# Expert stages of a two-block model: refills of the first weight slots issued in three parts, and one slot's place in the order of loads

## The reference, cut to what matters

```python
# hier_moe on n tokens h (512 tokens in layer 0, 256 in layer 1), top 2 experts of the best group
for each expert e and its tokens x:
    y = (silu(x @ w1[e]) * (x @ w3[e])) @ w2[e]
    out[token] += gate[token, e] * y
```

## Time and profile before

| | us |
|---|---|
| runs | 2123.81, 2121.19, 2123.91 (median 2123.81) |
| profiled execution | 2121.46, span 2119.7 |
| PE busy | 1903.6 (90% of the span) |
| DVE busy | 983.7 (46%) |
| DMA traffic | 610.65 MB, mean 288 GB/s |
| stage 0 of the experts | about 1035 to 1498 |
| stage 1 of the experts | about 1674 to the end |

### The profile page before, as it was taken

One profiled execution on the slowest core, in us unless ns is written; L12 is line 12 of the kernel. 1 busy time (PEld: TensorE's weight loads), 2 busy tenths in 40 slices (PEclk: granted clock), 3 DMA queues, 4 the chain that ended last, 5 costly groups with the idle time before them and its releaser, 6 DMA issues.

```text
span 2119.7 us, 22003 instructions
## 1 busy us (share of the span) xinstructions
PE 1903.6 (90%) x8957; PEld 1034.6 (49%) x8957; DVE 983.7 (46%) x1781; ACT 316.5 (15%) x717; POOL 37.7 (2%) x52
## 2 busy tenths in 40 slices
PE   8999999998999999999999999999999955455557
PEld 5558874455588745884643333333456511111112
DVE  3238878466378795646433333333765410110111
ACT  2121110226211103011200000000234200000000
POOL 0000000000000000000100000000000000000000
PEclk9999999999999999999999999999999977777789
DMA  9347886451278864421899999999722899999998
GB/s 367 137 142 265 288 297 219 146 184 41 81 270 285 296 222 161 138 101 40 345 429 426 427 426 426 427 427 423 276 80 99 313 425 427 426 426 426 427 426 338
DMA packets 147686, 610.65 MB, mean 288 GB/s; under 512 B 14609, under 2 KB 65489, under 8 KB 123136
## 3 DMA queue, kind: packets, MB, share of 16 engines
q1 hardware_dynamic: 141920, 595.87, 71.7%
q0 software_dynamic: 5568, 13.24, 1.7%
q10 hardware_dynamic: 96, 0.10, 0.0%
HBM read 610.62 MB, written 4.33 MB: 290 GB/s over the span
## 4 chain that ended last, share of the span: by engine, by line
PE 78%; DMA 15%; DVE 3%; ACT 2%; issue 1%; SPq 1%; DVEq 0%
PE psum L1071 14%; PE psum L2701 14%; PE psum L524 9%; PE psum L2729 7%; DMA ring<-in_w 6%; PE psum L1011 6%; PE psum L2766 5%; PE psum L1890 4%; DMA arena<-in_w 4%; DMA consts<-in_w 3%; PE psum L566 3%; PE psum L1977 2%; DMA normed_t<-in_w 1%; PE psum L642 1%; PE psum L1366 1%
## 5 line engine op out<-in xcount | busy, mean ns | idle before, releaser
L1071 PE MATMUL psum<-normed_t,ring 128*128 128x256 f32 x1408 | 306.4, 380 | 0.0
L1071 PEld LDWEIGHTS psum<-normed_t,ring 128*128 128x128 f32 x1408 | 266.9, 190 | 43.5 <-issue 7.2
L2701 PE MATMUL psum<-ring,arena 128*32 128x512 f32 (+1 forms) x720 | 211.0, 670 | 63.3 <-DMA arena<-in_w 24.6
L923 DVE SCALAR_TENSOR_TENSOR arena<-ring,silu_c,arena 128x1024 f32<-128x1024 f32 x168 | 204.7, 1279 | 0.0
L524 PE MATMUL psum<-ring,normed_t 128*128 128x512 f32 x448 | 196.7, 596 | 2.1 <-issue 0.9
L3136 DVE TENSOR_TENSOR resid<-resid,psum 128x512 f32<-128x512 f32 x160 | 109.9, 688 | 184.5 <-PE psum L2766 184.5
L2701 PE MATMUL psum<-consts,arena 128*32 128x512 f32 (+1 forms) x288 | 146.9, 669 | 19.5 <-DMA arena<-in_w 19.5
L3144 DVE TENSOR_TENSOR scaled<-scaled,psum 128x512 f32<-128x512 f32 x24 | 16.5, 688 | 315.8 <-PE psum L2701 315.8
L524 PEld LDWEIGHTS psum<-ring,normed_t 128*128 128x128 f32 x448 | 84.0, 191 | 104.1 <-issue 103.2
L2701 PE MATMUL psum<-arena 128*32 128x512 f32 (+1 forms) x328 | 108.2, 651 | 28.7 <-DMA ring<-in_w 28.7
L2701 PEld LDWEIGHTS psum<-ring,arena 128*32 128x32 f32 (+1 forms) x720 | 56.5, 131 | 142.6 <-issue 142.6
(11 more groups left out here) (570 smaller groups left out, 2805.3 us busy)
## 6 DMA issues: line engine op xcount, KB each, us to landing
ring<-in_w SPq DMA_DIRECT2D x96, 2048.0 KB, 29.8
arena<-in_w SPq DMA_DIRECT2D x36, 2048.0 KB, 29.4
consts<-in_w SPq DMA_DIRECT2D x28, 2048.0 KB, 34.5
ring<-in_w_mod SPq DMA_DIRECT2D x24, 2048.0 KB, 7.8
ring<-in_ffn_w_up SPq DMA_DIRECT2D x44, 1024.0 KB, 7.7
normed_t<-in_w SPq DMA_DIRECT2D x18, 2048.0 KB, 30.1
ring<-in_ffn_w_down SPq DMA_DIRECT2D x10, 2048.0 KB, 8.0
ring<-in_ab_w_in SPq DMA_DIRECT2D x6, 2048.0 KB, 16.7
```

Of the source, the lines that this page charges most:

```text
L923: ins = dv.scalar_tensor_tensor(out=acc, in0=w, scalar=sc, in1=acc, op0=ALU.mult, op1=ALU.add)
L1071: m = pe.matmul(PS[:, b, 256 * hf:256 * hf + 256], w[:, hf, k, P * cc:P * cc + P], HT[:, k, 0:T], start=(k == 0), stop=(k == KC - 1))
L2701: m = pe.matmul(PS[r, 2 + q, :], self.XT[c % 2][k // 4][:, k % 4, r], self.weights(c, q, h, FE * k, FE), start=k == 0, stop=k == KC - 1)
```

## The change

1. The order of slots 8 and 9 in stage 1 is swapped: the three-part slot comes before "own4".
2. The refills of slots 0 to 3 for the first time (tiles `ns` to `ns + 3`) are issued in three parts: columns 0 to 511 (what k = 0 has read), 512 to 2047 (k = 1 to 3) and 2048 to 4095. Each part waits for a mark of its own: two new marks after k = 0 and k = 3 of the hidden products of turn 0, and the old one at the end. For each group of lanes SP issues the first part of every tile, then the second, then the third. `loaded` counts the two more transfers.
3. The lists are computed after k = 0 of the first hidden product instead of before it.

```diff
-                    self.homes = [..., "tables", "own3", "own4", "parts", "normed"]
+                    self.homes = [..., "tables", "own3", "parts", "own4", "normed"]
...
+            EARLY = (0, 512, 2048, 4096)
+
             def loaded(self, pe, c, q):
                 for h in range(self.lanes):
                     n = self.tile(c, q, h)
-                    pe.wait_ge(self.w_loaded[n % self.ns], 16 * len(self.slots[n % self.ns]) * (n // self.ns + 1))
+                    i, turn = n % self.ns, n // self.ns
+                    more = 2 if turn and i < 4 else 0
+                    pe.wait_ge(self.w_loaded[i], 16 * (len(self.slots[i]) * (turn + 1) + more))
+
+            def load_early(self, sp, n, part):
+                i, q = n % self.ns, (n - self.ns) // self.lanes
+                sp.wait_ge(sems["pe"], upto("pe", f"{self.L}.hid{2 * q + 1}.0" + (f".{part}" if part < 2 else "")))
+                cols = slice(self.EARLY[part], self.EARLY[part + 1])
+                sp.dma_start(self.slots[i][0][:, cols], self.source(n)[:, cols]).then_inc(self.w_loaded[i], 16)
...
-                for n in range(self.tiles):
+                for n in range(self.ns):
+                    self.load_weights(sp, n)
+                for first in range(self.ns, self.ns + 4, self.lanes):
+                    for part in range(3):
+                        for n in range(first, first + self.lanes):
+                            self.load_early(sp, n, part)
+                for n in range(self.ns + 4, self.tiles):
                     self.load_weights(sp, n)
...
+                    if c == 0 and k in (0, 3):
+                        p.step(m, f"{L}.hid{2 * q + 1}.0.{k // 3}")
+                    if between and k == 0:
+                        between()
...
-                    self.pe_hidden(te, c, 0)
+                    self.pe_hidden(te, c, 0, lists if c == 0 else None)
```

More of the change, by code:

```diff
@@ L2517, in __init__ @@
                     at_tables = CST[:, CONST_AT["axcos0"][0]:][:, 0:4096]
-                    self.homes = ["free", "own0", "own1", "own2", "mid", "top", "tables", "own3", "own4", "parts", "normed"]
+                    self.homes = ["free", "own0", "own1", "own2", "mid", "top", "tables", "own3", "parts", "own4", "normed"]
                     parts = [X[:, 2:4, :].rearrange("p t d -> p (t d)"), GB[:, 1, :], Z[:, 2048:3072]]
-                    self.slots = [DEAD[:, 3584:7680], own[0], own[1], own[2], mid, top, at_tables, own[3], own[4], parts, HTF]
+                    self.slots = [DEAD[:, 3584:7680], own[0], own[1], own[2], mid, top, at_tables, own[3], parts, own[4], HTF]
                     self.YW = [XSF[:, 0:1024], XSF[:, 272:400]]
@@ L2687, in pe_first, with pe_hidden @@
                     p.step(m, f"{L}.turn{hf}.0")
-            def pe_hidden(self, te, c, q):
+            def pe_hidden(self, te, c, q, between=None):
                 pe, p, L = te.eng, te.p, self.L
@@ L2845, in pe, with lists @@
                 te.banks = {}
[L2847 to L2854, removed]
+                def lists():
+                    pe.wait_ge(sems["dve"], upto("dve", f"{L}.hot"))
+                    te.take(5, "dve", f"{L}.list")
+                    choices = [(t, k) for t in range(self.nt) for k in range(2)]
+                    for t, k in choices:
+                        for h in range(self.lanes):
+                            m = pe.matmul(PS[self.cap * h:self.cap * h + self.cap, 5, 0:self.groups], self.HR[:, t, k, :],
+                                          self.OHT[:, t, k, h::self.lanes], start=(t, k) == choices[0], stop=(t, k) == choices[-1])
+                    p.step(m, f"{L}.lists")
                 for c in range(self.groups):
-                    self.pe_hidden(te, c, 0)
+                    self.pe_hidden(te, c, 0, lists if c == 0 else None)
                     if c >= 1 and self.nt == 2:
```

## The result

| | median, us | range | runs |
|---|---|---|---|
| before | 2121.19 | 2120.86 to 2123.91 | 5 |
| after | 2113.30 | 2112.11 to 2114.35 | 5 |

The ratio is 0.9949 [0.9937, 0.9961]: by this comparison the kernel is faster by 0.4 to 0.6%. The profiled execution took 2114.35 us (span 2112.5) where that of before took 2121.46 (span 2119.7).

What follows compares the result with a forecast made beforehand. PE bounds about 12 of 16 first-stage turns, transfers the rest and the second stage. Profiled 2121.5 - 5.2 - 2.0 = 2114.3, then 2116.6 because the median lay 2.35 above the profiled execution; range 2114.0 to 2121.5 us.

Steps and rivals of the forecast that it cites:

- Second stage: 5.2: Second expert stage: net gain of 5.2 us from reordered slots and refills in parts, bounds 4.1 and 6.3.
- the sooner issue: Second stage: first refill piece waits for k = 0 alone and is issued 6.3 us earlier, 1674.95 instead of 1681.29.
- the pieces' price: Second stage: 2 x 512 more packets from refills in parts cost 0.5 us, between nothing and 1.0.
- 2.1 and 3.0 us of idle time: Second stage: DMA idle time by shares in the holes at 1655 to 1660 and 1678 to 1683, 5.1 us together.
- the hole by bytes: Second stage: holes sized by bytes missing against the full rate, 2.9 + 3.8 = 6.7 us.
- First stage: 2.0: First expert stage: refills in parts gain 2.0 us by removing PE's waits for weights, bounds 0 and 2.3.
- the turn of 29.19 us: First stage: one turn of the loop over `c`, all PE work, taken as what PE needs without waits.
- B: First stage: turn 1's row gather takes 11 us, PE stalls 2.3 us, stage gains nothing: 2118.9 us; chance 0.20.
- E: First stage: gather lands 17 us after issue, 8.3 us after PE needs it; kernel slower, 2124.9 us; chance 0.06.
- Rival C: Second stage: reordered tile brings nothing, preloads end with the normed tile anyway; 2119.3 us in all; chance 0.13.
- Rival D: SP held in its order, or pieces pay double price; both stages end almost as before, 2121.3 us; chance 0.09.
- The wait for tile 11: Second stage: tile 11 complete about 1689 to 1690, before its output product begins at 1690.5; delay would cost nothing.

Runs made afterwards that it cites:

- second profile: The kernel after, unchanged, measured once more against before: 2115.57 us, ratio 0.9963; stage 1 took 443.87 us.
- order_only: Against before, only the new order of the two slots in stage 1, refills whole and lists first: 2123.97 us, ratio 1.0003; stage 1 took 448.41 us.
- lists_first: The kernel after with the lists back before k = 0: 2115.15 us, ratio 0.9965 to before.

## Why the prediction was right and where it failed

**What failed is the base.** The prediction put: "The median of the runs shown, 2123.81, is 2.35 above it, within their spread (2121.19 to 2123.91), so 2116.6." That step set a right difference on a wrong base. By the profiled execution the forecast was 2114.3, and the profiled execution of after took 2114.35. But of the three runs behind 2123.81 two were high; with two more beside the runs of after, the median of before is 2121.19, 0.27 below its own profiled execution, and the median of after is 1.05 below its own. Without the 2.35 us the forecast is 1.0 above the measured 2113.3 instead of 3.3. The range had the same fault: it held the uncertain gain and not the uncertain base, and its lower end, 2114.0, lay 0.7 us above the result. That the base moves is shown: before had 2121.19 in one comparison and 2124.06 in another, and the kernel after 2113.30 and 2115.57 beside them. So subtracting something from the profiled execution would not have been safe either; the range needed some 2 us for the base on the low side. That 2114.3 and 2114.35 agree so well is in part luck: the start of the expert stages moves by up to 9 us between executions of the same code, and in these two profiles it was 0.35 us apart. The gain itself, 7.2 us, is what the profiles gave (7.11); the medians gave 7.9 and 8.5.

**Second stage: 5.2, and 5.22 came (5.68 in the second profile).** Of its terms, the sooner issue was 6.3 as forecast and the pieces' price 0.6 instead of 0.5. The order was worth 1.1 us alone and 1.0 or 1.4 on top of the pieces (445.32 less the two profiles of after), the pieces 4.2 alone; the prediction read 2.1 and 3.0 us of idle time. It gave the order too much, since the hole it closes is handed on in part to the next gate (order_only). It gave the pieces too little: even the hole by bytes, 3.8 less 0.6, makes 3.2, and what the last us is, is open. The two errors have opposite signs, so the hit of the sum is in part luck. One step of its argument was also misread, at no cost: the 7.4 us "still queued" at 1681.2 are the whole length of the second piece; by the prediction's own times about 4 of them were left.

**First stage: 2.0, and 2.27 came.** The sum took the turn of 29.19 us for what PE needs, but that turn was itself late by 0.07: the turns ahead of it take 29.11 to 29.14 in both kernels, so those gained nothing. The four turns from 1335.57 to 1454.08 took 118.51 us and take 116.49 now (1335.92 to 1452.41), which is 2.02 instead of the 1.75 of the sum, and the last turn gave the 0.25 that were forecast.

**The gather (rivals B and E)** was forecast 7 us to landing and took 8.0 (issued at 1040.24), with 1.1 us to spare before the product that needs it starts, and no wait for it:

```profile
arena<-expert_inputs,token_of_slot POOLq DMA_INDIRECT x1, 8.0
```

```profile
1049.35 1.09 PE L2690 MATMUL psum<-consts,arena 128*128 128x128 f32 x8
```

Rival C, the order brings nothing, fell as a whole time, but it was half right: the order alone brought 1.1 of the 2.1 us. Rival D fell with SP's issue times: the longest among the pieces were 1.78 and 1.19 us, within the row of 1676.32, and the third piece still went out while the second had work until 1687.

**The wait for tile 11 was sized wrong, without a price.** Tile 11 was to be complete at 1689 to 1690, before an output product begins. The product could have started at 1687.8 and waited 4.33 us:

```profile
1692.14 1.03 PE L2749 MATMUL psum<-resid,consts 128*32 128x512 f32 x1 [4.33 <-DMA consts<-in_w]
```

It cost nothing that shows, for the reason given: the hidden product behind it waits for weights anyway, and started at 1704.85, before the 1708 that was forecast.

**The lists** cost nothing on either side (lists_first).

## What to carry to other kernels

In a stage that is bound by transfers, add up the idle time of the transfer engines from its preloads to its steady stream: each us of it was worth about a us here (within 1 us in all) if it isn't handed on to the next wait, and a transfer cut in pieces that follow the reader's columns takes it back for 0.15 us for each 2 MB tile in three pieces. Before moving a tile ahead of one gate, list all gates that follow, for the gap moves to the next one unless that one is opened too. Predict the difference, and hang it on a base only as exactly as that is known: here two medians of one kernel were 2.3 to 2.9 us apart, as much as the whole correction that was made.

## What was not expected of the hardware

- The first packets of a transfer that reaches the engines soon after its issue are slow, and the share of busy time hides it. After: 1676 to 1680 has a share of 0.99 and 267 GB/s.

```profile
1676.00:1680.00 4.00, 4.00 (x40) 1.34 (x36) 3.59 (x18) 0.60 (x1) 2.05 (x2) 1.00 0.99 267
```

  These are the 6 KB packets of the second piece, issued at 1675.95: 1066 ns on average from 1677 to 1678, 501 in the next us, 274 in the third, and 234 in the steady stream. The engines were busy until then (a share of about 1 from 1676 to 1677, in 2 KB packets), so idle time just before is not needed for it. The 2 KB packets of the first piece took 84 ns at the median from their start, and the 8 KB packets of the third, issued at 1679.85 and begun 7 us later, 309 to 325 from the first on. Before the change the 16 KB packets issued at 1681.29 took 1349 ns on average in the first us and 611 later. So the end of a hole costs more than its idle share.
- The time of one packet on one engine in a full stream: 84 to 88 ns for 2 KB, 159 to 162 for 4 KB, 234 for 6 KB, 309 to 313 for 8 KB, 611 to 614 for 16 KB, about 11 ns and 75 ns for each 2 KB.
- The 0.5 MB gather (a single one, or the first of a pair) took 3.4 to 4.4 us in a hole, 7.6 to 9.3 beside packets of up to 8 KB and 10.0 to 11.9 beside those of 16 KB, over five of the kernels. Its landing time goes with the size of its neighbours' packets.
- The same code of the first 1025 us takes up to 9 us longer from one execution to the next: up to 6.4 with the granted TensorE clock of 20 us of sparse attention, up to 2.7 with the first feed-forward product.
